# A three-block network on one core: order of ScalarE, VectorE and bank waits in three seven-product MLPs

## The chip, the cores and the metric

One Trainium2 chip, one core. The time is the device time of one launch in microseconds, the median of the runs; a trace of one profiled execution stands beside it. The kernel works in fp32 precision built from fp32r (rounded) operands: each factor is split into a rounded high part and the rest as low part, and a product is three matmuls (high by high, high by low, low by high).

## The reference

512 tokens of width 1024 go through three networks one after the other; five of their parts are MLPs. Cut to what the change touches:

```
squared_relu_mlp(h, w_in, w_out) = square(relu(h @ w_in)) @ w_out          # first block, twice: mlp0, mlp1 (hidden 4096)
gate, up = h @ w_gate, h @ w_up;  (silu(gate) * up) @ w_down                # second block: ffn1, ffn2 (hidden 2816); third: ffn3
h = rms_norm(x, g)                 # ahead of mlp0, mlp1, ffn1, ffn2
mod = silu(c) @ w_ada + b_ada      # conditioning vector of the third block, 1024 -> 6 * 1024
```

The change touches mlp1, ffn1 and ffn3. Between mlp1 and ffn1 nothing stands; ahead of ffn3 stands the third block's first layer norm.

## The kernel before, in words

Activations are kept turned, 128 features by 512 tokens a tile. Each engine has its own program, written out in order by hand, and engines meet only at semaphores (`e.wait_ge`, named by `P`, `C`, `D`, `G` for TensorE, ScalarE, VectorE, GpSimd). SyncE issues all weight loads in one order (`sync`), into three raw slabs in turn: load i waits until the slab of load i - 3 has been read (`raw_free`). GpSimd goes through the same list in `gpsimd`.

An MLP's hidden tiles are worked in groups of four, of which the last of ffn1 and ffn3 has two. Group 0 is done in the ordinary way (`lin`), by TensorE under two-tile steps `p0` = 0 and 2. From group 1 on the three MLPs named use a seven-product (Strassen-Winograd) form: a 1024x256 weight block times 512 tokens is cut 2x2, and seven products of half size replace eight. One **step** of TensorE is `pair_pe` (seven products of 12 matmuls with 256 columns, in the order b, a, c, b, m, c, b over three regions in three PSUM banks) and then `outs_pe` (the down projection of the group before: m output tiles of 12 matmuls with 512 columns). mlp1 has 14 steps with m = 4; ffn1 and ffn3 have 16 steps with m = 2, a gate and a value step in turn, and 2 with m = 4. A step takes 3 + m of the six banks of ring `ps`, each freed by who read it last.

Round the products stands this work. Steps are counted from 0 in each MLP; s is the one that TensorE is in.
- **GpSimd**: `pair_sums_pool` makes the four sums S1, S3, S2, S4 of the weight blocks of a coming pair; `outs_low_pool` makes the low parts of the m output tiles.
- **ScalarE**, `paired_act` for step s: seven high parts of the weight blocks of step s + 1 (`pair_high_act`, a generator, so that `some(high, n)` issues n of them; order A11, A12, S1, S2, A22, S4, S3); m high parts of the down weights of step s (`outs_high_act`); four copies of partial sums out of PSUM (`pair_parts_act`, in the order P1, P5, U2, P4); and two high parts of the hidden tiles or two Silu (`hidden`). Product 3 of TensorE waits for P1, product 5 for P5, product 6 for U2.
- **VectorE**, `paired_dve` for step s: the m adds of the down results of step s - 1 into x; seven low parts of the weights of step s + 1, which free that slab; the hidden low parts; `pair_first_dve` and `pair_second_dve`, which free banks 0 and 1 of the pair; `made`.
- **The conditioning slabs.** In mlp0, mlp1 and ffn1 w_ada is multiplied by the way in 36 parts: parts 0 and 1 of each three load a 1 MB slab (`ada_pe`) and VectorE reads it in four instructions into `macc` (`ada_dve`); part 2 is eight small matmuls of TensorE in a bank of `ps` and one small add. In mlp1 a part belongs to every step, in ffn1 to every second.
- **The opening.** `token_sums_dve` makes four sums of the tokens from ScalarE's scaled copies (`pairs_begin_act`); `pairs_high_act`, `pairs_low_dve`, `pairs_open_act` and `pairs_open_dve` split them and the first pair's weights. `roots_act` and `roots_dve` make rb, 1 / rms of each token. In ffn3 the copies are made in the layer norm.

The order of ScalarE in one step, as the kernel before has it (lines 1901 to 1917):

```
some(parts, opens)
self.outs_high_act(a, o)
some(high, 1)
some(parts, not opens)
some(high, 1 if opens else 2)
... hidden or Silu ...
some(parts, 1); some(high, 2); some(parts, 1); some(high, 1); some(parts, 1); run(high)
```

Of the kernel before, what the change touches and what calls it, by code (L numbers as in the profile page):

```python
# [221 lines left out]
class Net:  # L222
# [152 lines left out]
    def pair_pe(self, e, key, W, c0, after=None, first=False):  # L375
# [6 lines left out]
        self.pair_at[s] = i, q  # L382
        banks = []
        for n in range(3):
            bank, free = self.ps.take(key, n)
            e.wait_ge(*free)
            banks.append(bank)
        a, c, b, m = banks[0][:, 0:256], banks[0][:, 256:512], banks[1][:, 0:256], banks[2][:, 0:256]
        for n, out in enumerate((b, a, c, b, m, c, b)):
            e.wait_ge(*D.at("low", s, n))  # L390
            if first and n in (2, 3, 4, 6):
                e.wait_ge(*D.at(key[0], "tokens", n))
            if n == 3:
                e.wait_ge(*C.at(key, "P1"))
            elif n == 5:
                e.wait_ge(*C.at(key, "P5"))
            elif n == 6:
                e.wait_ge(*C.at(key, "U2"))
            hi, lo = self.piece(self.whi, q + n), self.piece(self.wlo, q + n)
            for k in range(4):  # L400
                xh, xl = self.token_block(n, k)
                e.mm(out, hi[:, k, :], xh, k == 0 and n in self.OPENS, False)
                e.mm(out, hi[:, k, :], xl, False, False)
                t = e.mm(out, lo[:, k, :], xh, False, k == 3 and n in self.CLOSES)
            t.then_inc(*P.up(key, "product", n))
            self.piece_free[q + n] = P.now()
# [1349 lines left out]
    def mlp_pe(self, e, name, gate, up, down, nt, T, ada, between=None, opening=None, last=None):  # L1756
# [39 lines left out]
        for g in range(len(groups) + 1):  # L1796
# [3 lines left out]
            if g < len(groups):  # L1800
                first(g)
                if g == len(groups) - 1:
                    self.P.mark("used", name)
                if ada:
                    self.ada_pe(e)
# [82 lines left out]
    def paired_act(self, a, name, gated, T, g, groups):  # L1888

        D, some = self.D, self.some  # L1890
        hidden = self.hidden_high_act if gated else self.relu_squares_act
        for j, kind, p0, s, o, before, opens, ends, _ in self.pair_steps(name, gated, g, groups):
# [5 lines left out]
            else:  # L1898
                last = "made" if gated else "h"
                parts = self.pair_parts_act(a, key, *(T["gt"][i] for i in pair), *(D.at(name, last, g - 1, i) for i in pair))  # L1900
            some(parts, opens)
            self.outs_high_act(a, o)
            some(high, 1)
            some(parts, not opens)
            some(high, 1 if opens else 2)
            if before:
# [5 lines left out]
            some(parts, 1)  # L1912
            some(high, 2)
            some(parts, 1)
            some(high, 1)
            some(parts, 1)
# [5 lines left out]
    def paired_dve(self, d, name, gated, T, g, groups, add, ada):  # L1922
# [30 lines left out]
        for j, kind, p0, s, o, before, opens, ends, m in self.pair_steps(name, gated, g, groups):  # L1953
# [9 lines left out]
            if before:  # L1963
                for i in range(before[1], before[1] + 2):
                    hidden(d, name, T, before[0], i)
            some(low, 2 if kind == "gate" or not gated else 1)
            self.pair_first_dve(d, key, m1)
# [7 lines left out]
            run(low)  # L1975
            if ada and m * (j + 1) % 4 == 0:
                self.ada_dve(d)
# [5 lines left out]

    def pairs_begin_act(self, a, name, gain):

        a.wait_ge(*self.D.at(f"n{name}", 7))
        for k in range(8):
            a.f(self.tok_t["v"][k // 4][:, k % 4, :], self.x[:, k, :], ACT.Copy, scale=gain(k)).then_inc(
                *self.C.up(name, "token value", k))

    def pairs_high_act(self, a, name):
# [52 lines left out]
    def mlp_act(self, a, name, gated, nt, T, rooted, squares, nxt, extra=None):  # L2044
        groups, way = self.mlp_groups(nt), self.pairing.get(name)
        for g in range(len(groups)):
            if extra:
                extra(g)
            if way and g:
                self.paired_act(a, name, gated, T, g, groups)  # L2050
                continue
            if way and way.gain:
                self.pairs_begin_act(a, name, way.gain)
            for p0 in range(0, len(groups[g]), 2):
# [56 lines left out]
    def mlp_dve(self, d, name, gated, nt, T, add, rooted, squares, ada, nxt, turns=None, amid=None):  # L2111
        P, C, D = self.P, self.C, self.D
        groups, way = self.mlp_groups(nt), self.pairing.get(name)
        for g in range(len(groups) + 1):
# [3 lines left out]
            if g < len(groups):  # L2118
                for p0 in range(0, len(groups[g]), 2):
                    if way and p0 == (0 if way.gain else 2):  # L2120
                        self.token_sums_dve(d, name)
                    if way and p0:
                        low = self.pairs_low_dve(d, name)
                    if gated:
# [5 lines left out]
                if way:  # L2130
                    self.pairs_open_dve(d, name, low)
                if ada:
                    self.ada_dve(d)
# [28 lines left out]
    def relu_mlp_act(self, a, l, nxt, last=None):  # L2162
        name = f"mlp{l}"
        self.roots_act(a, f"n{name}", False)
        self.mlp_act(a, name, False, 32, self.mlp1_t[l], True, True, nxt)
        if last:
            last()
        self.barrier(a, self.C, name)

    def relu_mlp_dve(self, d, l, nxt, amid=None):  # L2170
        name = f"mlp{l}"
        self.roots_dve(d, f"n{name}", False)
        add = lambda d, n, bank, out: d.tt(out, self.x[:, n, :], bank[:, :], ADD)
# [399 lines left out]
    def ffn2_act(self, a, name, nxt):  # L2573
        if name == "ffn2":
            a.dma(self.m3["sp"][:, :], self.A["ssm"]).then_inc(*self.small_in["ssm"].up("ssm"))
        self.roots_act(a, f"n{name}", False)
        self.mlp_act(a, name, True, 22, self.mlp1_t[0], True, name == "ffn1", nxt,
# [5 lines left out]

    def ffn2_dve(self, d, name, nxt):
        self.roots_dve(d, f"n{name}", False)
        add = lambda d, n, bank, out: d.stt(out, bank[:, :], 0.5, self.x[:, n, :], MUL, ADD)
# [2330 lines left out]
```

## Time and profile before

| | us |
|---|---|
| median of 3 runs | 3482.66 (3479.57 to 3490.39) |
| the profiled execution | 3486.54 |
| its span in the trace | 3484.60 |
| TensorE busy | 3300.6 (95%) |
| VectorE, GpSimd, ScalarE busy | 2096.4, 1800.4, 1114.4 |
| mean granted TensorE clock | 0.986 |

Busy shares are means over the whole span, and a busy TensorE isn't TensorE at its peak; for this change the stretches of the three MLPs are read one by one (mlp1 about 940 to 1355 us, ffn1 1355 to 1760, ffn3 3128 to 3472).

### The profile page before, as it was taken

To read this page: it belongs to the slowest core of one execution; us is meant where nothing else is said; L and a number is where in the kernel's file an instruction comes from. 1 tells how busy PE (TensorE), PEld (TensorE's weight loads), DVE (VectorE), ACT (ScalarE), POOL (GpSimd) and SP (SyncE) were. 2 spreads that over 40 slices of the span, in tenths; PEclk is the share of its full clock that TensorE was granted. 3 is DMA by queue.
4 is the path that set the end of the run, shared out by engine and by line. 5 is a ranking of instruction groups with operands and counts; after the bars stand their busy time and mean duration, and the time that the engine had idled before them with its cause. 6 is when DMAs were issued, how large, how long until landed. Compare 5 with 4: busy or idle time off the path is not lost.

```text
span 3484.6 us, 51536 instructions
## 1 busy us (share of the span) xinstructions
PE 3300.6 (95%) x21318; PEld 2714.0 (78%) x21318; DVE 2096.4 (60%) x3132; ACT 1114.4 (32%) x2317; POOL 1800.4 (52%) x1387
## 2 busy tenths in 40 slices
PE   8999999999969899789999998899999999999998
PEld 7768788976758787688978778778887776768997
DVE  6554443467477776678763366554345666658775
ACT  2241111357434433344412442110002116234543
POOL 7526567640344446345676100666664744836562
PEclk9999999999989999899999999999999999999999
DMA  5212333220122323233333100432332735412331
GB/s 178 74 37 97 133 124 130 87 79 13 37 97 97 133 97 103 79 103 103 109 99 114 56 2 15 145 98 91 97 97 89 239 110 182 157 55 85 109 113 52
DMA packets 262153, 341.08 MB, mean 98 GB/s; under 512 B 10016, under 2 KB 202784, under 8 KB 259360
## 3 DMA queue, kind: packets, MB, share of 16 engines
q1 hardware_dynamic: 239408, 301.51, 26.7%
q10 hardware_dynamic: 22512, 36.28, 3.0%
q8 instruction: 169, 2.77, 0.3%
q14 instruction: 64, 0.52, 0.0%
HBM read 308.15 MB, written 25.43 MB: 96 GB/s over the span
## 4 chain that ended last, share of the span: by engine, by line
PE 78%; DVE 13%; DMA 4%; ACT 3%; issue 1%; POOL 1%; ACTq 0%; SPq 0%; DVEq 0%; POOLq 0%
PE bank L130 76%; DVE wlo L153 2%; DMA raw<-in_w_mlp_in 2%; DVE macc L163 2%; PE bank L133 2%; DVE scr L153 1%; DMA sq<-gates 1%; DMA raw<-in_ffn_w_up 1%; DVE gt L153 1%; ACT whi L148 0%; DMA raw<-in_ffn_w_gate 0%; DVE x L153 0%; DVE hl L153 0%; DVE gt L163 0%; DVE st L168 0%
## 5 line engine op out<-in xcount | busy, mean ns | idle before, releaser
L153 POOL TENSOR_TENSOR wlo<-raw,whi 128x512 fp32r<-128x512 f32 x762 | 1058.4, 1417 | 350.5 <-ACT whi L148 337.3
L130 PE MATMUL bank<-ah,whi 128*128 128x512 f32 (+1 forms) x2408 | 872.8, 362 | 67.2 <-ACT gt L148 33.1
L160 POOL TENSOR_SCALAR whi<-raw 128x1024 fp32r<-128x1024 f32 x313 | 361.0, 1171 | 1057.9 <-PE bank L130 543.9
L130 PE MATMUL bank<-ah,wlo 128*128 128x512 f32 (+1 forms) x2408 | 863.2, 358 | 0.0
L130 PE MATMUL bank<-al,whi 128*128 128x512 f32 (+1 forms) x2408 | 851.8, 359 | 0.9 <-DVE al L163 0.9
L130 PEld LDWEIGHTS bank<-ah,whi 128*128 128x128 f32 x2408 | 456.6, 190 | 158.7 <-DVE wlo L153 36.9
L130 PEld LDWEIGHTS bank<-al,whi 128*128 128x128 f32 x2408 | 456.4, 190 | 77.4 <-DVE al L163 1.8
L130 PEld LDWEIGHTS bank<-ah,wlo 128*128 128x128 f32 x2408 | 456.1, 189 | 73.8 <-issue 0.2
L130 PE MATMUL bank<-hh,whi 128*128 128x512 f32 x1040 | 412.6, 397 | 0.5 <-DVE hl L153 0.5
L130 PE MATMUL bank<-hl,whi 128*128 128x512 f32 x1040 | 410.9, 395 | 0.0
L130 PE MATMUL bank<-hh,wlo 128*128 128x512 f32 x1040 | 410.8, 395 | 0.0
L148 ACT ACTIVATE whi<-raw 128x512 fp32r<-128x512 f32 x336 | 204.7, 626 | 313.0 <-PE bank L130 130.4
L153 DVE TENSOR_TENSOR wlo<-raw,whi 128x512 fp32r<-128x512 f32 x200 | 214.3, 1087 | 89.3 <-ACT whi L148 89.2
L130 PEld LDWEIGHTS bank<-hh,whi 128*128 128x128 f32 x1040 | 195.2, 188 | 48.2 <-issue 2.2
L130 PEld LDWEIGHTS bank<-hh,wlo 128*128 128x128 f32 x1040 | 195.0, 187 | 47.6
L130 PEld LDWEIGHTS bank<-hl,whi 128*128 128x128 f32 x1040 | 195.2, 188 | 44.8
L130 PE MATMUL bank<-h,whi 128*128 128x256 f32 x600 | 176.2, 294 | 45.9 <-ACT gt L148 39.2
L130 PE MATMUL bank<-l,whi 128*128 128x256 f32 x600 | 173.7, 289 | 0.0
L130 PE MATMUL bank<-h,wlo 128*128 128x256 f32 x600 | 173.5, 289 | 0.0
L163 DVE SCALAR_TENSOR_TENSOR x<-bank,x 128x512 f32<-128x512 f32 x112 | 74.5, 685 | 141.0 <-PE bank L130 140.7
L130 PEld LDWEIGHTS bank<-h,whi 128*128 128x128 f32 x600 | 118.9, 198 | 49.6 <-ACT gt L148 36.0
L153 POOL TENSOR_TENSOR sq<-raw 128x512 f32<-128x512 f32 x50 | 78.2, 1564 | 145.1 <-DMA raw<-in_w_mlp_in 67.2
(484 smaller groups left out, 5459.3 us busy)
## 6 DMA issues: line engine op xcount, KB each, us to landing
raw<-in_w_in SPq DMA_DIRECT2D x34, 1024.0 KB, 5.3
raw<-in_w_mlp_in SPq DMA_DIRECT2D x32, 1024.0 KB, 5.6
raw<-in_w_mlp_out SPq DMA_DIRECT2D x32, 1024.0 KB, 7.6
raw<-in_w_ada SPq DMA_DIRECT2D x24, 1024.0 KB, 5.4
raw<-in_ffn_w_gate SPq DMA_DIRECT2D x22, 1024.0 KB, 5.4
raw<-in_ffn_w_up SPq DMA_DIRECT2D x22, 1024.0 KB, 5.4
raw<-in_w_ffn_in SPq DMA_DIRECT2D x22, 1024.0 KB, 6.2
raw<-in_w_out SPq DMA_DIRECT2D x16, 1024.0 KB, 5.5
```

Of the source, the lines that this page charges most:

```text
L130: return self.eng.matmul(out, lhsT, rhs, start=start, stop=stop, skip_group_check=True)
L133: return IDLE if self.eng is None else self.eng.transpose(out, src, ident)
L148: return self.eng.activation(out, src, func, scale=scale, **kw)
L153: return IDLE if self.eng is None else self.eng.tensor_tensor(out, a, b, op)
L160: return self.eng.tensor_scalar(out, a, s1, s2, op0, op1)
L163: return IDLE if self.eng is None else self.eng.scalar_tensor_tensor(out, a, s, b, op0, op1)
```

## The change

In all three MLPs:
- `pair_pe` takes its three banks at once but waits for them singly: bank 1 ahead of product 0, bank 0 ahead of product 1, bank 2 ahead of product 4.
- `paired_act`: P1 is copied first in every step. In the first step (`opens`) no high part of the next pair stands ahead of the last copy P4; in the others the numbers of high parts between the copies are 1, 0, 2, 2 and the rest, where they were 1, 2, 2, 1 and the rest.
- `paired_dve`: a part of the conditioning that reads a slab is done after the hidden low parts, in the middle of the step, where it stood at the step's end. Part 2 stays at the end.

In mlp1 and ffn1:
- group 0 has no part of the conditioning any more; all later parts move one place back (a load in the list too).
- ScalarE's eight scaled copies of the tokens and VectorE's four token sums stand ahead of the root, where they stood behind it.

```diff
--- before.py
+++ after.py
@@ -380,13 +380,11 @@
         s, self.n_pair = self.n_pair, self.n_pair + 1
         q = self.pieces(7)
         self.pair_at[s] = i, q
-        banks = []
-        for n in range(3):
-            bank, free = self.ps.take(key, n)
-            e.wait_ge(*free)
-            banks.append(bank)
+        banks, free = zip(*(self.ps.take(key, n) for n in range(3)))
         a, c, b, m = banks[0][:, 0:256], banks[0][:, 256:512], banks[1][:, 0:256], banks[2][:, 0:256]
         for n, out in enumerate((b, a, c, b, m, c, b)):
+            if n in (0, 1, 4):
+                e.wait_ge(*free[{0: 1, 1: 0, 4: 2}[n]])
             e.wait_ge(*D.at("low", s, n))
             if first and n in (2, 3, 4, 6):
                 e.wait_ge(*D.at(key[0], "tokens", n))
@@ -1801,7 +1799,7 @@
                 first(g)
                 if g == len(groups) - 1:
                     self.P.mark("used", name)
-                if ada:
+                if ada and not way:
                     self.ada_pe(e)
             if g:
                 second(g - 1)
@@ -1898,11 +1896,9 @@
             else:
                 last = "made" if gated else "h"
                 parts = self.pair_parts_act(a, key, *(T["gt"][i] for i in pair), *(D.at(name, last, g - 1, i) for i in pair))
-            some(parts, opens)
+            some(parts, 1)
             self.outs_high_act(a, o)
-            some(high, 1)
-            some(parts, not opens)
-            some(high, 1 if opens else 2)
+            some(high, not opens)
             if before:
                 for i in range(before[1], before[1] + 2):
                     hidden(a, name, T, before[0], i)
@@ -1910,9 +1906,9 @@
                 for i in pair:
                     self.paired_silu_act(a, name, T, g, i)
             some(parts, 1)
-            some(high, 2)
+            some(high, 0 if opens else 2)
             some(parts, 1)
-            some(high, 1)
+            some(high, 0 if opens else 2)
             some(parts, 1)
             run(high)
             if ends:
@@ -1963,6 +1959,10 @@
             if before:
                 for i in range(before[1], before[1] + 2):
                     hidden(d, name, T, before[0], i)
+            part = ada and m * (j + 1) % 4 == 0
+            if part and self.ada_d % 3 < 2:
+                self.ada_dve(d)
+                part = False
             some(low, 2 if kind == "gate" or not gated else 1)
             self.pair_first_dve(d, key, m1)
             if kind == "gate":
@@ -1973,7 +1973,7 @@
             self.pair_second_dve(d, key, m2)
             made(kind, p0, p0 + 1, m2)
             run(low)
-            if ada and m * (j + 1) % 4 == 0:
+            if part:
                 self.ada_dve(d)
         if ends:
             for i in (p0, p0 + 1):
@@ -1981,12 +1981,20 @@
                 hidden(d, name, T, g, i)
             adds(g - 1, 8 - m + 2, m - 2)
 
-    def pairs_begin_act(self, a, name, gain):
-
+    def pairs_begin_act(self, a, name):
+
+        if name not in self.pairing:
+            return
+        gain = self.pairing[name].gain
         a.wait_ge(*self.D.at(f"n{name}", 7))
         for k in range(8):
             a.f(self.tok_t["v"][k // 4][:, k % 4, :], self.x[:, k, :], ACT.Copy, scale=gain(k)).then_inc(
                 *self.C.up(name, "token value", k))
+
+    def pairs_begin_dve(self, d, name):
+
+        if name in self.pairing:
+            self.token_sums_dve(d, name)
 
     def pairs_high_act(self, a, name):
 
@@ -2049,8 +2057,6 @@
             if way and g:
                 self.paired_act(a, name, gated, T, g, groups)
                 continue
-            if way and way.gain:
-                self.pairs_begin_act(a, name, way.gain)
             for p0 in range(0, len(groups[g]), 2):
                 if way and p0:
                     high = self.pairs_high_act(a, name)
@@ -2117,9 +2123,9 @@
                 continue
             if g < len(groups):
                 for p0 in range(0, len(groups[g]), 2):
-                    if way and p0 == (0 if way.gain else 2):
-                        self.token_sums_dve(d, name)
                     if way and p0:
+                        if not way.gain:
+                            self.token_sums_dve(d, name)
                         low = self.pairs_low_dve(d, name)
                     if gated:
                         self.gated_dve(d, name, T, g, range(p0, min(p0 + 2, len(groups[g]))), p0, rooted, not (way and p0))
@@ -2129,7 +2135,7 @@
                         turns(g)
                 if way:
                     self.pairs_open_dve(d, name, low)
-                if ada:
+                if ada and not way:
                     self.ada_dve(d)
             if g:
                 end = g == len(groups)
@@ -2161,6 +2167,7 @@
 
     def relu_mlp_act(self, a, l, nxt, last=None):
         name = f"mlp{l}"
+        self.pairs_begin_act(a, name)
         self.roots_act(a, f"n{name}", False)
         self.mlp_act(a, name, False, 32, self.mlp1_t[l], True, True, nxt)
         if last:
@@ -2169,6 +2176,7 @@
 
     def relu_mlp_dve(self, d, l, nxt, amid=None):
         name = f"mlp{l}"
+        self.pairs_begin_dve(d, name)
         self.roots_dve(d, f"n{name}", False)
         add = lambda d, n, bank, out: d.tt(out, self.x[:, n, :], bank[:, :], ADD)
         self.mlp_dve(d, name, False, 32, self.mlp1_t[l], add, True, True, True, nxt, amid=amid)
@@ -2573,6 +2581,7 @@
     def ffn2_act(self, a, name, nxt):
         if name == "ffn2":
             a.dma(self.m3["sp"][:, :], self.A["ssm"]).then_inc(*self.small_in["ssm"].up("ssm"))
+        self.pairs_begin_act(a, name)
         self.roots_act(a, f"n{name}", False)
         self.mlp_act(a, name, True, 22, self.mlp1_t[0], True, name == "ffn1", nxt,
                      (lambda g: {2: self.ssm_sines_act, 3: self.ssm_cosines_act}.get(g, lambda a: None)(a))
@@ -2582,6 +2591,7 @@
         self.barrier(a, self.C, name)
 
     def ffn2_dve(self, d, name, nxt):
+        self.pairs_begin_dve(d, name)
         self.roots_dve(d, f"n{name}", False)
         add = lambda d, n, bank, out: d.stt(out, bank[:, :], 0.5, self.x[:, n, :], MUL, ADD)
         if name == "ffn2":
```

## Rows read from the trace of the kernel before

**Rows 1.** The page: engines; the chain that ended last, by engine.

```profile
PE 3300.6 (95%) x21318; PEld 2714.0 (78%) x21318; DVE 2096.4 (60%) x3132; ACT 1114.4 (32%) x2317; POOL 1800.4 (52%) x1387
...
PE 78%; DVE 13%; DMA 4%; ACT 3%; issue 1%; POOL 1%; ACTq 0%; SPq 0%; DVEq 0%; POOLq 0%
```

**Rows 2.** Stretches in mlp1, ffn1, ffn3: length; busy PE, PEld, DVE, ACT, POOL; PEclk; DMA.

```profile
1014.58:1309.08 294.50, 266.31 (x1617) 235.54 (x1617) 215.65 (x241) 119.54 (x228) 135.98 (x96) 0.98 0.34 115
1437.72:1613.32 175.60, 151.04 (x989) 139.59 (x988) 136.12 (x147) 65.74 (x136) 89.42 (x57) 0.93 0.31 100
3178.26:3409.26 231.00, 231.00 (x1621) 214.49 (x1620) 171.25 (x193) 112.22 (x226) 136.16 (x92) 1.00 0.32 104
```

**Rows 3.** TensorE in mlp1: start us, length, what, [idle before].

```profile
1040.77 0.36 PE L130 MATMUL bank<-ah,whi 128*128 128x256 f32 x1 [1.54 <-DVE x L153]
...
1187.87 0.36 PE L130 MATMUL bank<-ah,whi 128*128 128x256 f32 x1 [1.54 <-DVE x L153]
...
1197.84 0.40 PE L130 MATMUL bank<-hh,whi 128*128 128x512 f32 x1
...
1209.04 0.28 PE L130 MATMUL bank<-ah,whi 128*128 128x256 f32 x1
```

**Rows 4.** TensorE at the openings: mlp1, ffn1 (three rows), ffn3.

```profile
970.51 0.55 PE L130 MATMUL bank<-ah,whi 128*128 128x256 f32 x1 [6.84 <-DVE wlo L153]
...
998.01 0.55 PE L130 MATMUL bank<-ah,whi 128*128 128x256 f32 x1 [17.79 <-ACT gt L148]
...
1381.66 0.79 PE L130 MATMUL bank<-ah,whi 128*128 128x512 f32 x1 [3.72 <-DVE gt L153]
...
1426.31 0.55 PE L130 MATMUL bank<-ah,whi 128*128 128x256 f32 x1 [11.55 <-ACT gt L148]
...
1432.12 0.40 PE L130 MATMUL bank<-hh,whi 128*128 128x512 f32 x1
...
3169.81 0.55 PE L130 MATMUL bank<-h,whi 128*128 128x256 f32 x1 [5.18 <-ACT gt L148]
```

**Rows 5.** ScalarE, opening of mlp1 and two steps in it.

```profile
953.17 5.01 ACT L148 ACTIVATE v<-x,par 128x512 f32<-128x512 f32 x8
...
994.08 1.15 ACT L148 ACTIVATE whi<-raw 128x512 fp32r<-128x512 f32 x2 [18.03 <-DMA raw<-in_w_mlp_in]
...
1042.45 0.39 ACT L148 ACTIVATE gt<-bank 128x256 f32<-128x256 f32 x1 [3.02 <-PE bank L130]
1042.73 0.62 ACT L148 ACTIVATE whi<-raw 128x512 fp32r<-128x512 f32 x1
...
1068.74 0.63 ACT L148 ACTIVATE whi<-raw 128x512 fp32r<-128x512 f32 x1 [8.86 <-DMA raw<-in_w_mlp_in]
```

**Rows 6.** VectorE: opening of mlp1; a contended and a lone low part; a slab read.

```profile
953.31 3.35 DVE L175 RECIPROCAL rb<-rb 128x512 f32<-128x512 f32 x1 [6.99 <-ACT rb L148]
...
963.09 1.28 DVE L163 SCALAR_TENSOR_TENSOR gt<-bank,rb 128x512 f32<-128x512 f32 x2
...
1047.67 0.69 DVE L153 TENSOR_TENSOR wlo<-sq,whi 128x512 fp32r<-128x512 f32 x1
...
1054.75 4.25 DVE L163 SCALAR_TENSOR_TENSOR macc<-raw,mc,macc 128x512 f32<-128x512 f32 x3
...
1072.16 1.77 DVE L153 TENSOR_TENSOR wlo<-sq,whi 128x512 fp32r<-128x512 f32 x1
```

**Rows 7.** SyncE, issue of loads in mlp1.

```profile
986.32 0.50 SPq L123 DMA_DIRECT2D raw<-in_w_mlp_in  x1
...
1059.44 0.51 SPq L123 DMA_DIRECT2D raw<-in_w_mlp_in  x1
```

**Rows 8.** GpSimd: a lone and a contended low part.

```profile
1051.68 1.29 POOL L153 TENSOR_TENSOR wlo<-raw,whi 128x512 fp32r<-128x512 f32 x1 [7.33 <-ACT whi L148]
...
1077.99 1.79 POOL L153 TENSOR_TENSOR wlo<-raw,whi 128x512 fp32r<-128x512 f32 x1 [2.91 <-ACT whi L148]
```

**Rows 9.** The page, loads: KB each, median us from issue to landing.

```profile
raw<-in_w_mlp_in SPq DMA_DIRECT2D x32, 1024.0 KB, 5.6
```

## The prediction

> **What bounds the kernel now.** The page comes first: TensorE is busy for 95% of the span and carries 78% of the chain that ended last, VectorE 13% and loads 4% [rows 1]. So the gain to be had is TensorE's idle time inside the three MLPs, not engine work as such. Second, the busy times by stretch [rows 2] say how much there is. ffn3, 15 steps with m = 2 and no conditioning, is 231.00 us of 231.00 busy at full clock: 15.40 us is the floor of such a step. ffn1's steps 1 to 9 take 175.60 us against 9 x 15.40 + 2 x 0.8 (part 2 of the conditioning, below) = 140.2: 35.4 us lost, at a granted clock of 0.93. For mlp1 the floor is read from one undisturbed step [rows 3]: products from 1187.87 to 1197.84, outs to 1209.04, so 21.17 us. Its steps 1 to 12 take 294.50 us against 12 x 21.17 + 4 x 0.8 = 257.2: 37.3 us lost. Third, the idle times with who ended them [rows 4]: the openings hold 6.84 and 17.79 us (mlp1), 3.72 and 11.55 (ffn1) and 5.18 (ffn3). The long ones all end with a copy of a partial sum by ScalarE, and ScalarE itself was waiting for a load: 18.03 us ahead of 994.08, 8.86 ahead of 1068.74 [rows 5]. It stands in its own order behind a high part of the next pair (`some(high, 1)`), while TensorE wants P1 of this one. And the loads were late because their slab turn came after VectorE's read of a conditioning slab: that read runs from 1054.75 for 4.25 us, and the next pair's load is issued at 1059.44 [rows 6, 7]. So the chain is read, load, high part, P1, product 3.
>
> **Token sums moved up.** In mlp1 ScalarE's eight copies take 5.01 us from 953.17 [rows 5]. x is complete before that, and VectorE is idle for 6.99 us ahead of the reciprocal at 953.31 [rows 6]. Behind it, the wait for the copies and the four sums fill the 6.4 us from 956.66 to the first relu at 963.09. Done ahead, copies and sums (5 us each) end near 955.3, the reciprocal (3.35) at 958.7, the relu comes at 958.9: 4.2 us earlier, and all of the opening with it. TensorE's 6.84 becomes 2.6. In ffn1 the same move makes the 3.72 us vanish: its work runs beside a group 0 that is long enough.
>
> **P1 first, no high part in the opening step.** The wait for P1 (17.79 us in mlp1) goes. What is late next: `outs_pe` of step 0 needs the hidden low parts of tiles 2 and 3, which VectorE makes behind three low parts of pair 1. In mlp1 pair 1's slab is pair 0's. It is issued at 986.32 now [rows 7], behind a slab read of some 3 us, so pair 0 was read at about 983; 4.2 us sooner, less 1 us of contention, is 979.7. With the median of 5.6 us [rows 9] it lands at 985.3; A11, A12, S1 and the hidden parts, high and low, are eight instructions and take about 5.1 more, 990.4. TensorE ended product 4 at 980.2 (998.01 less 17.79); 4.2 sooner, and with products 5 and 6 (held by the last low part) and two rows of outs, it gets there at 981.6: 8.8 us idle in place of 17.79. Gain of mlp1's opening 4.2 + 9.0, less 0.7 for a start at the lower clock level (1.2 in place of 2.4 GHz) that falls on outs in place of products: **12.5** (9 to 17). In ffn1 no conditioning load stands ahead any more, pair 1's slab is there early, and 11.55 becomes about 2.3. After that idle TensorE took 5.81 us (1426.31 to 1432.12) for two products [rows 4], where two of seven in rows 3 take 2.8; most of that comes back too. 3.7 + 9.2 + 2.7 = **15.6** (11 to 18). In ffn3 5.18 goes and about 1 of slow clock, and 1.2 of a new wait for the hidden parts comes: **+5**.
>
> **The steps of mlp1.** Count from TensorE's product 0. P1 can be copied at 1.68 (1042.45 less 1040.77) [rows 3, 5]; ScalarE's next instruction follows 0.28 later, by the rows then a 512-column copy each 0.54 us (0.62 long, overlapping) and a hidden tile 1.2. What it loses by the new order: the down weights' high parts, which it now does beside the outs of the step before, wait behind P1. So they run at 1.96 to 4.2, A11 at 4.1, hidden parts to 7.0, P5 at 7.05 (product 5 wants it at 7.1), A12 to 7.9, and then S1. GpSimd is queued behind that: its four low parts start at 2.6, at 1.29 each lone and 1.79 contended [rows 8], then it makes S1. U2 stands behind S1's high part, at 9.9 to 10.6, where product 6 could start at 8.45. That is a **new wait of 1.5 to 3.2 us in each step**; I take 2.2, near the lone price, as VectorE has little to do just then. The banks: bank 2 waits for an add of VectorE that product 4 wants 5.6 us later, so 0.58 us goes; after part 2 the ring is shifted by one, bank 1 itself waits for an add behind the small one, and of the 1.54 us [rows 3] 0.9 stays, with 0.8 for the eight matmuls. Loads: the slab read in mid-step (4.25 us plus one of about 0.5) no longer ends ahead of a load that the next step wants. In one step of three it now delays the later low parts, so that pair s + 2 is issued at 22 us of the step and lands near 5 of the next, under the S1 wait. 12 x (21.17 + 2.2) + 4 x 1.7 = 287.2 against 294.50: **7.3** (stall 1.5: 16; stall 3.2: -5). Step 13 has no part 2 any more: **+1**.
>
> **The steps of ffn1 and ffn3.** Here only two low parts stand ahead of S1. GpSimd starts at 2.6, S1 ends at 6.5 lone, 7.35 with the contended times; U2 at 7.4 to 8.3, wanted at 8.45: just hidden, and P5 at 4.6 long before. VectorE has 15 instructions a step and 4 more with a slab read, 13 and 18 us with contention; the 5 us of a read are made up in the next step. A pair that needs its forerunner's slab lands up to 6 us into the step: 1 us. Steps 1 to 9: 140.2 + 4 = 144.2 against 175.60: **31.4** (1.7 us a step left: 20; floor: 35). Later in ffn1 two reads fall into steps that lose nothing today: **-1.5**. Step 16 in ffn1 and ffn3 has m = 4 and gets mlp1's wait: **-1.9** each. ffn3's other steps: 0, with no cover against a late S1 (0.3 us a step: -5; nothing to gain, they are at the floor).
>
> GpSimd's low part takes 1.79 in place of 1.29 beside VectorE's work, and VectorE's 1.77 in place of 0.69 [rows 6, 8]. The Trainium skill, "SBUF — State Buffer", section "Who interferes with whom", says that a VectorE instruction with two SBUF inputs and a GpSimd one that reads SBUF lock each other out for a whole instruction. Rows and rule agree on the loser's side for VectorE. By the rule GpSimd could lose a whole VectorE instruction each time, which the change invites, as it moves GpSimd's down parts into the first half of the step; the last rival says what that would give.
>
> **Sum.** 12.5 + 7.3 + 1 + 15.6 + 31.4 - 1.5 - 1.9 + 5 - 1.9 = 67.5 us. The profiled execution took 3486.54 us, of which 3484.60 are the span; it is 3.88 above the median of the runs, 3482.66. I take the difference over to the median: 3482.66 - 67.5 = **3415**.
>
> **Rivals.**
> (a) The steps keep their losses, only the openings gain: 12.5 + 15.6 + 5 = 33, so 3450. That is so if U2 is gated by the load as P1 was: A11, A12 and S1 of the next pair stand ahead of U2, and a slab that lands later than 7 us into a step stops TensorE just as before. For it: 8.86 us of waiting for a load in rows 5. Against it: that load was issued behind a slab read, which is out of the way. Chance 0.15.
> (b) mlp1's steps reach their floor: 12 x 21.17 + 4 x 1.7 = 260.8, 26 us more, 3389. It needs U2 before 8.45, with five GpSimd operations of 1.29 or more from 2.6 on ahead of it: 9.05. Only if ScalarE's down parts didn't wait for P1. Chance 0.08.
> (c) Slower. GpSimd loses time of VectorE's ahead of each operation. At 0.69 each, U2 comes at 13.4 in mlp1 (stall 5.0, 34 us more than I have) and at 9.5 in the 32 steps with m = 2 (1.05 each, 34 us): the gain is gone, no change. It decides from there: at 0.9 each it is 5 x 0.2 x 12 + 3 x 0.2 x 32, 31 us slower, 3514. For it: ffn3 runs without any idle time today because these parts are done a step ahead. Against: the rows show 0.5 at most, and VectorE waits for ScalarE then. Chance 0.05.
> (d) It does nothing that can be told from no change, since the loads and reads only change places: 3483. Against: the waits of rows 4 name ScalarE's copies. Chance 0.03.
>
> **Range and chances.** The forecast has 0.69. The ends of its terms, taken together, would give 15 to 93 us; all at one end is unlikely, and 40 to 90 us is my range: 3393 to 3443. It leaves out (a), half of (b) and (c), (d). A measurement of this kernel can tell about 0.3% from no change, 10.4 us: faster 0.92, same 0.03, slower 0.05.
>
> **What the changed profile would show.** Right: no idle time over 3 us ahead of a copy by ScalarE, but one of about 9 in mlp1's step 0 that ends with a hidden low part (hl); no wait of 3.7 at ffn1's group 0; in mlp1 an idle of about 2 us in each step, between products 5 and 6, ended by a ScalarE copy; steps of 23.4 in mlp1 and 15.4 to 16 in ffn1; ffn3's steps still 15.4. Wrong: idle time ahead of product 6 in ffn3 (then (c)), or ScalarE waiting for loads in every step (then (a)), or mlp1's steps at 21.2 (b).

## The result and the profile after

The changed kernel takes **3457.27 us** (median of 4 runs, 3448.42 to 3460.81) against 3481.52 us before (4 runs): ratio 0.9922, 95% interval 0.9896 to 0.9947. That is 24 to 27 us faster, where 67.5 were forecast and 40 to 90 were the range: the direction is right, the size wrong by a factor of 2.5 to 2.8. The profiled execution took 3448.42 us, the fastest of its four and 9 us under their median (span 3446.5); it is 38 us under the one of before. Of these, 31 lie in the three MLPs. The other 7 lie between ffn1 and ffn3, where the trace of before takes 1429.2 us from ffn1's last step to ffn3's first, and all thirteen other traces 1421.4 to 1423.4. Two of the thirteen, e2 and e11, are the kernel before with one edit inside the MLPs, so I count the 7 us as no effect of the change.

The page of the kernel after, engines and chain:

```profile
PE 3295.1 (96%) x21318; PEld 2701.5 (78%) x21318; DVE 2036.9 (59%) x3132; ACT 1105.2 (32%) x2317; POOL 1803.1 (52%) x1387
...
PE 76%; DVE 11%; POOL 5%; ACT 4%; DMA 2%; issue 1%; ACTq 0%; DVEq 0%; SPq 0%; POOLq 0%
```

Against [rows 1] the loads' share of the chain has halved (4% to 2%), and GpSimd, 1% before, has 5%. The same stretches as in [rows 2], here steps 1 to 12 of mlp1, 1 to 9 and 10 to 16 of ffn1, 1 to 15 and 16 of ffn3 (length; busy PE, PEld, DVE, ACT, POOL; PEclk; DMA share, GB/s):

```profile
1003.60:1299.84 296.24, 267.37 (x1617) 233.45 (x1616) 192.58 (x240) 115.06 (x228) 140.31 (x96) 0.99 0.36 113
1410.11:1565.47 155.36, 146.62 (x989) 134.00 (x988) 118.67 (x144) 65.42 (x135) 82.25 (x54) 0.98 0.34 109
1565.47:1691.07 125.60, 117.58 (x789) 107.00 (x788) 97.76 (x119) 51.94 (x107) 66.97 (x44) 0.99 0.36 118
3131.39:3366.53 235.14, 233.44 (x1621) 215.51 (x1620) 156.71 (x193) 108.89 (x225) 136.69 (x90) 1.00 0.32 104
3366.53:3391.67 25.14, 22.80 (x134) 20.19 (x132) 15.16 (x19) 8.29 (x17) 11.70 (x8) 0.93 0.25 84
```

Term by term, in us (the traces; "before" is the length in the trace of before):

| | before | after | forecast gain | measured gain |
|---|---|---|---|---|
| mlp1, opening to step 1 | | | 12.5 | 11.0 |
| mlp1, steps 1-12 | 294.50 | 296.24 | 7.3 | -1.7 |
| mlp1's end and ffn1's opening | 128.64 | 110.27 | 1 + 15.6 | 18.4 |
| ffn1, steps 1-9 | 175.60 | 155.36 | 31.4 | 20.2 |
| ffn1, steps 10-16 | 113.49 | 125.60 | -3.4 | -12.1 |
| ffn3, step 0 | 22.27 | 18.93 | 5 | 3.3 |
| ffn3, steps 1-15 | 231.00 | 235.14 | 0 | -4.1 |
| ffn3, step 16 | 21.00 | 25.14 | -1.9 | -4.1 |

The openings came in the size that was worked out, 32.7 of 34.1 us. The steps were to give 33.4 net and gave -1.9. TensorE's idle times in the kernel after: mlp1's opening, a wait for U2 and one for a hidden low part in its steps, a value step of ffn1, step 16 of ffn3:

```profile
992.08 0.80 PE L130 MATMUL bank<-hh,whi 128*128 128x512 f32 x1 [9.48 <-DVE hl L153]
...
1014.42 0.39 PE L130 MATMUL bank<-h,whi 128*128 128x256 f32 x1 [1.88 <-ACT gt L148]
...
1092.00 0.50 PE L130 MATMUL bank<-hh,whi 128*128 128x512 f32 x1 [0.73 <-DVE hl L153]
...
1451.87 0.39 PE L130 MATMUL bank<-ah,whi 128*128 128x256 f32 x1 [2.62 <-ACT scr L148]
...
3377.44 0.36 PE L130 MATMUL bank<-h,whi 128*128 128x256 f32 x1 [2.35 <-ACT gt L148]
```

And what ScalarE, GpSimd and VectorE do in mlp1's step 1, which TensorE begins at 1003.60 (first ScalarE, then GpSimd, then VectorE):

```profile
1005.20 0.39 ACT L148 ACTIVATE gt<-bank 128x256 f32<-128x256 f32 x1 [12.54 <-PE bank L130]
1005.48 2.70 ACT L148 ACTIVATE whi<-raw 128x512 fp32r<-128x512 f32 x5
...
1013.47 0.63 ACT L148 ACTIVATE whi<-sq 128x512 fp32r<-128x512 f32 x1 [2.12 <-POOL sq L153]
1014.00 0.37 ACT L148 ACTIVATE gt<-bank 128x256 f32<-128x256 f32 x1
```

```profile
1006.25 5.51 POOL L153 TENSOR_TENSOR wlo<-raw,whi 128x512 fp32r<-128x512 f32 x4 [14.77 <-ACT whi L148]
1011.72 1.72 POOL L153 TENSOR_TENSOR sq<-raw 128x512 f32<-128x512 f32 x1
```

```profile
1014.13 1.20 DVE L153 TENSOR_TENSOR wlo<-sq,whi 128x512 fp32r<-128x512 f32 x1 [1.82 <-ACT whi L148]
1015.25 3.48 DVE L153 TENSOR_TENSOR hl<-gt,hh 128x512 fp32r<-128x512 f32 x2
```

Counted from the start of the step, P1 is copied at 1.6 us, GpSimd's four low parts run until 8.2 and its sum S1 until 9.8; the high part of S1 follows at 9.9 and U2 at 10.4. That chain is as forecast. What the forecast didn't follow is the lower half: VectorE's low part of S1 and, behind it in VectorE's order, the two hidden low parts, done at 1018.73, 15.1 us into the step. In every second step of mlp1 `outs_pe` wants them in that same step; in four of the twelve steps TensorE waits for them, 0.60 to 0.73 us each.

### The profile page after: what moved, and what is told of

Its sections match the earlier page's. It is cut to its first block, busy times and chain, and to the rows that moved or that the text cites. A ratio compares the mean times of both kernels' runs of the same rounds, so it can differ in the third digit from the quotient of the medians.

```text
span 3446.5 us, 51330 instructions
## 1 busy us (share of the span) xinstructions
PE 3295.1 (96%) x21318; PEld 2701.5 (78%) x21318; DVE 2036.9 (59%) x3132; ACT 1105.2 (32%) x2317; POOL 1803.1 (52%) x1387
## 4 chain that ended last, share of the span: by engine, by line
PE 76%; DVE 11%; POOL 5%; ACT 4%; DMA 2%; issue 1%; ACTq 0%; DVEq 0%; SPq 0%; POOLq 0%
PE bank L130 74%; POOL wlo L153 3%; DVE wlo L153 2%; PE bank L133 2%; ACT whi L148 1%; DVE hl L153 1%; DVE scr L153 1%; POOL sq L153 1%; DMA raw<-in_ffn_w_gate 1%; ACT gt L148 1%; POOL whi L160 1%; DVE macc L163 0%; DVE st L168 0%; DMA raw<-in_w_mlp_in 0%; ACT ah L148 0%
## 5 line engine op out<-in xcount | busy, mean ns | idle before, releaser
L153 DVE TENSOR_TENSOR wlo<-raw,whi 128x512 fp32r<-128x512 f32 x200 | 179.3, 901 | 145.9 <-ACT whi L148 145.7
L148 ACT ACTIVATE whi<-raw 128x512 fp32r<-128x512 f32 x336 | 195.6, 620 | 30.3 <-DMA raw<-in_ffn_w_gate 18.0
L153 DVE TENSOR_TENSOR wlo<-sq,whi 128x512 fp32r<-128x512 f32 x100 | 104.2, 1045 | 87.8 <-ACT whi L148 87.2
```

Source lines behind the costliest of these rows:

```text
L148: return self.eng.activation(out, src, func, scale=scale, **kw)
L153: return IDLE if self.eng is None else self.eng.tensor_tensor(out, a, b, op)
```

## The experiments

Two theories. **T1**: a late S1 is what the new order of ScalarE costs, and the gain of the change comes from the slab read in mid-step. **T2**: late slabs bound the steps; the order of ScalarE is right. Ratios are to the kernel before, run beside them. Differences to the changed kernel are of medians that weren't run side by side, and the changed kernel's own interval is 9 us to either side (its four runs lie 12 us apart), so differences of 10 us or so are read from the traces.

### e1: down parts ahead of P1 again

```diff
-            some(parts, 1)
+            some(parts, opens)
             self.outs_high_act(a, o)
+            some(parts, not opens)
             some(high, not opens)
```

> The changed kernel with one thing moved: in all but the opening steps ScalarE makes the high parts of the down weights ahead of P1 again (the order is down parts, P1, A11, ...). Theory T1 (the new wait for U2 comes from the down parts behind P1: they hold up GpSimd's low parts and with them the sum S1 that stands ahead of U2): the wait of 1.86 us ahead of product 6 goes, mlp1's steps 1 to 12 take about 268 us in place of 296, ffn3's steps 1 to 15 take 231 in place of 235.1 and step 16 takes 21 in place of 25.1, some 40 to 50 us less than the changed kernel in all, about 3412. Theory T2 (late slabs of the next pair bound the steps): the wait moves from U2 to a load, mlp1's steps stay over 285 us, the whole is within 10 us of the changed kernel, about 3450.

Measured 3406.40 us, ratio 0.9787 (0.9771 to 0.9804), 51 us under the changed kernel. The same five stretches:

```profile
1002.88:1270.33 267.45, 258.09 (x1618) 229.78 (x1616) 205.40 (x244) 117.53 (x228) 135.79 (x96) 1.00 0.38 127
1379.03:1529.74 150.71, 144.55 (x989) 133.39 (x987) 132.34 (x147) 66.12 (x135) 86.19 (x54) 0.98 0.33 111
1529.74:1651.49 121.75, 118.41 (x788) 108.61 (x789) 108.83 (x121) 54.37 (x109) 74.75 (x46) 0.97 0.36 124
3094.98:3325.98 231.00, 231.00 (x1622) 214.47 (x1620) 161.88 (x194) 109.40 (x227) 142.45 (x92) 1.00 0.32 105
3325.98:3346.98 21.00, 21.00 (x134) 18.79 (x132) 13.25 (x17) 8.82 (x17) 12.78 (x9) 1.00 0.28 101
```

In the step that begins at 1071.81, GpSimd's S1, then ScalarE's high part of S1 and U2:

```profile
1075.15 1.29 POOL L153 TENSOR_TENSOR sq<-raw 128x512 f32<-128x512 f32 x1 [3.94 <-DMA raw<-in_w_mlp_in]
```

```profile
1078.81 0.62 ACT L148 ACTIVATE whi<-sq 128x512 fp32r<-128x512 f32 x1
1079.33 0.37 ACT L148 ACTIVATE gt<-bank 128x256 f32<-128x256 f32 x1
```

U2 is copied 7.5 us into the step in place of 10.4, ahead of product 6. All T1's numbers for the steps (268, 231, 21) are met. The place of the down parts alone is worth 51 us by the medians, 47 by the ratios, 44 by the traces.

### e2 and e3: ScalarE's new order alone, and everything but it

e2 is the kernel before with the new `paired_act`; e3 the changed kernel with the old one:

```diff
-            some(parts, 1)
+            some(parts, opens)
             self.outs_high_act(a, o)
-            some(high, not opens)
+            some(high, 1)
+            some(parts, not opens)
+            some(high, 1 if opens else 2)
...
             some(parts, 1)
-            some(high, 0 if opens else 2)
+            some(high, 2)
             some(parts, 1)
-            some(high, 0 if opens else 2)
+            some(high, 1)
```

> The kernel before with ScalarE's new order in paired_act alone. T1: the openings gain the waits for P1 (some 25 us over the three), the steps of mlp1 gain nothing, since their wait moves to U2, and ffn3 loses 8 us as in the changed kernel; 3460 to 3468. T2: the old slab reads at the step's end keep each load late, P5 and U2 wait for it, and the gain is under 10 us, 3475.

> The changed kernel with the old order of ScalarE in paired_act; slab reads, token sums and bank waits stay as changed. T1: the loads come early enough now, so the old order costs little in the steps: no wait for S1 ahead of U2, ffn3's steps at 231.0 again, mlp1's near 275; the openings lose some 15 us against the changed kernel; in all 3440, better than the changed kernel. T2: P1 waits for the load behind A11 again as in the kernel before, 3470.

e2: 3513.36 us, ratio 1.0091 (1.0076 to 1.0107), **32 us slower** than before; both theories missed it. Its steps 1 to 12 of mlp1 take 312.54 us, and its opening of mlp1 gives next to nothing (step 1 starts 42.9 us after product 0, 44.1 before): the slab read still stands ahead of pair 1's load and the hidden parts behind it. That is the likely reason; no run takes it apart. e3: 3404.18 us, ratio 0.9782 (0.9768 to 0.9797), **53 us faster than the changed kernel**, beyond what T1 gave it (by the traces 46; the changed kernel was traced in its fastest run). So the new order costs 32 us on the old kernel and about 50 on the new. e3's stretches, the first four:

```profile
1003.69:1265.04 261.35, 257.26 (x1617) 230.10 (x1616) 199.81 (x240) 120.22 (x228) 131.99 (x96) 1.00 0.40 133
1376.21:1526.87 150.66, 143.48 (x990) 132.65 (x989) 131.38 (x147) 65.46 (x134) 84.80 (x53) 0.99 0.35 116
1526.87:1647.62 120.75, 116.86 (x789) 107.86 (x788) 106.69 (x119) 54.97 (x109) 74.26 (x46) 0.97 0.36 118
3093.32:3324.98 231.66, 231.66 (x1622) 215.18 (x1621) 170.83 (x193) 112.36 (x226) 136.18 (x91) 1.00 0.32 103
```

With A11 ahead of P1, as before, mlp1's steps are at 21.8 us on average, 33 us under before in all: the load that A11 waits for is there.

T1 had e3's openings 15 us behind those of the changed kernel; that missed. mlp1's step 1 starts at 1003.69 us in e3 and at 1003.60 in the changed kernel. Over the three openings the gain on the kernel before is, by the traces:

| | mlp1 | mlp1's end and ffn1 | ffn3 | sum |
|---|---|---|---|---|
| changed kernel | 11.0 | 18.4 | 3.3 | 32.7 |
| e3, without ScalarE's new order | 10.9 | 17.5 | -0.2 | 28.2 |
| e2, with ScalarE's new order alone | 1.2 | 1.8 | 3.3 | 6.4 |
| e12 (below), e3 with a part of the conditioning in group 0 | 2.2 | 7.8 | -0.1 | 9.9 |

So nearly all of the gain in the openings of mlp1 and ffn1 comes from the empty group 0 and the earlier token sums, and only that of ffn3 from ScalarE's order.

### e5, e6, e7, e12: the other parts, each taken back from e3

```diff
# e5: the slab read at the end of the step
-            if part and self.ada_d % 3 < 2:
-                self.ada_dve(d)
-                part = False
# e6: all three banks ahead of product 0
+        for f in free:
+            e.wait_ge(*f)
...
-            if n in (0, 1, 4):
-                e.wait_ge(*free[{0: 1, 1: 0, 4: 2}[n]])
# e7: the calls of pairs_begin_act and pairs_begin_dve back behind the root
# e12: a part of the conditioning in group 0
-                if ada and not way:
+                if ada:
```

> The changed kernel with the old order of ScalarE (as e3) and besides with the slab reads of the conditioning at the end of the step again. Token sums, bank waits and the missing part in group 0 stay. T1 (the gain of the change is the slab read, which stood ahead of the next pair's load; ScalarE's copies were only where the wait showed): most of e3's gain goes, 40 to 50 us slower than e3's 3404, about 3450. T2 (the openings and the banks carry it): within 15 us of e3.

> e3 with all three banks waited for ahead of product 0 again. T1: bank 2 then waits for an add of VectorE in two of three steps of mlp1 (0.58 us each in rows 3's steps) and after part 2 0.6 us more; 5 to 10 us slower than e3. T2 (with reads in mid-step VectorE is late at the step's end, so the bank waits matter more): 15 us or more slower.

> e3 with the token copies and sums behind the root again in mlp1 and ffn1. T1: mlp1's opening 3 to 4 us and ffn1's group 0 3.7 us later: 7 us slower than e3, 3411. T2 (the opening waits for a load anyway, so this is hidden): within 2 us of e3.

> e3 with a part of the conditioning in group 0 again (so a slab load and its read ahead of pair 1's load in the openings). T1: mlp1's opening 3 us and ffn1's up to 6 us longer, 3410. T2 (the load of pair 1 waits for pair 0 in any case): within 3 us of e3, 3404.

| | us | ratio to before (95%) | worth beside e3 |
|---|---|---|---|
| e5, read at the end | 3461.08 | 0.9944 (0.9928 to 0.9961) | 57 |
| e6, banks together | 3416.71 | 0.9819 (0.9805 to 0.9834) | 13 |
| e7, sums behind the root | 3414.85 | 0.9808 (0.9794 to 0.9823) | 11 |
| e12, part in group 0 | 3416.04 | 0.9816 (0.9799 to 0.9833) | 12 |

All four fall on T1's side, each with a larger price than T1 gave (40 to 50, 5 to 10, 7, and 6 us). The interval of e7 overlaps that of e3 (0.9768 to 0.9797), but its trace has the loss where T1 put it: 2.9 us by mlp1's step 1, 5.6 between mlp1's steps and ffn1's product 0. By the traces e12 loses 18 us in the openings and 5 in ffn1's steps 1 to 9, and wins 7 back in its steps 10 to 15.

Who waited in steps 1 to 12 of mlp1 (us in total, times, longest), e5 and then the changed kernel:

```profile
ACT whi L148 <- DMA raw<-in_w_mlp_in: 72.0, 12, 8.8
...
PE bank L130 <- ACT gt L148: 21.2, 12, 3.4
```

```profile
ACT whi L148 <- POOL sq L153: 48.3, 24, 2.5
...
PE bank L130 <- ACT gt L148: 21.8, 15, 1.9
...
PE bank L130 <- DVE hl L153: 2.7, 4, 0.7
```

TensorE's waits name the same pair of engines with nearly the same sum, 21 to 22 us. What ScalarE itself waited for tells them apart: in e5 a load, in the changed kernel GpSimd's sums. The wait says who came last, not why.

### e11: the slab read in mid-step alone, in the kernel before

> The kernel before with the slab read of the conditioning in mid-step and nothing else. T1: this alone brings most of what the parts beside ScalarE's order bring, 45 to 55 us of the 76, 3430. T2 (it works only with the bank waits and the empty group 0): under 30 us, 3455.

3434.05 us, ratio 0.9867 (0.9851 to 0.9883): 46 us faster. One statement moved ten lines up in `paired_dve` beats the whole change by about 20 us (23 by the medians, 19 by the ratios).

### e4, e9, e10: who waits for the late S1

e4 puts the hidden low parts ahead of the low parts of A12 and S1 (in the opening ahead of A11 too), e9 puts U2 ahead of the high part of S1, e10 does both; the down parts stay behind P1 in all three.

```diff
# e4, in paired_dve
-            some(low, 3)
+            some(low, 0 if opens else 1)
             if before:
                 ... hidden ...
+            some(low, 3 if opens else 2)
# e9, in paired_act
-            some(high, 0 if opens else 2)
+            some(high, 0 if opens else 1)
             some(parts, 1)
-            some(high, 0 if opens else 2)
+            some(high, 0 if opens else 3)
```

> The changed kernel with the two hidden low parts of a step moved ahead of VectorE's low parts of A12 and S1 (in the opening step ahead of all three). T1 (TensorE's waits for hl stand behind S1's low part): the waits ended by hl go, 9.5, 2.6 and 3.3 us in the three openings and about 8 us in the steps; bank 0 then is the next in mlp1's opening and gives back about 4; 3438 to 3445. T2 (hl is late because of load and port, not of the order): under 5 us less than the changed kernel, 3453.

> The changed kernel (down parts behind P1 as changed) with one high part in place of two between P5 and U2, so that U2 stands ahead of the high part of S1; three follow it. T1 (S1 is late behind the down parts; it has two victims, U2 on ScalarE and the hidden low parts on VectorE, which stand behind S1's low part): the wait of 1.86 ahead of product 6 goes, but in every second step of mlp1 the outs wait for hl, some 3 us, since those parts are no earlier; about 15 us less than the changed kernel, 3440. T2 (U2 is the only victim): 30 us less or more, 3425.

> e9 and besides the hidden low parts ahead of VectorE's low parts of A12 and S1 (as in e4). T1: both victims of a late S1 are out of its way, so most of what e1 gave comes back although the down parts still stand behind P1: mlp1's steps near 22, about 3415 to 3420. T2 (GpSimd is late in the step as such, and the loads and later parts hang on it too): within 10 us of e9.

e4: 3444.11 us, ratio 0.9896 (0.9881 to 0.9911), 13 under the changed kernel. e9: 3447.35, ratio 0.9907 (0.9891 to 0.9922), 10 under. Both intervals overlap that of the changed kernel (0.9896 to 0.9947), so neither gain is clear of noise. e10: **3405.91**, ratio 0.9791 (0.9772 to 0.9810), 51 under, which is. Steps 1 to 12 of mlp1 in e4 and in e10, as above:

```profile
1000.72:1307.74 307.02, 274.56 (x1618) 241.65 (x1616) 221.62 (x241) 114.81 (x228) 147.58 (x96) 0.96 0.35 112
```

```profile
1001.74:1276.04 274.30, 260.80 (x1618) 230.43 (x1617) 216.11 (x239) 114.86 (x228) 145.22 (x96) 1.00 0.38 123
```

The changed kernel takes 296.24 there, e9 293.61. So for mlp1's steps e4 alone is 11 us worse (its waits for U2 grew from 21.8 to 27.8 us; why wasn't tried; its openings are 8.5 us shorter), e9 alone 3 better, and the two together 22 better: S1 has two waiters, and with one helped the other holds TensorE. TensorE's waits in steps 1 to 12 of mlp1, e9:

```profile
PE bank L130 <- DVE hl L153: 11.0, 9, 1.7
PE bank L130 <- DVE gt L153: 5.3, 4, 1.5
PE bank L130 <- ACT gt L148: 4.1, 3, 2.0
```

From 21.8 the waits for ScalarE fall to 4.1, but hl rises from 2.7 to 11.0 and a bank that VectorE frees adds 5.3. In e10 no wait for hl is left there. e1 and e10 are two different ways round the same sum, and both get back most of what the new order costs; that is the strongest evidence for T1. That their times agree within 1 us is luck: e10's steps 1 to 12 of mlp1 are 7 us longer than e1's (267.45), and its openings, where it moves the hidden parts too, are 8 us shorter. S1's lateness is not cured in e10, and 7 us of it still show.

### e8: e1 with the opening's hidden parts first

```diff
-            some(low, 3)
+            some(low, 0 if opens else 3)
             if before:
                 ... hidden ...
+            some(low, 3 if opens else 0)
```

> e1 (down parts ahead of P1) and besides in the three opening steps VectorE's two hidden low parts ahead of its low parts of the next pair. T1: the waits for hl in the openings go; as in e4 3 to 3.5 us less in mlp1's and ffn1's opening and 2 in ffn3's, 8 us less than e1: 3398, faster than both kernels. T2 (bank 0, whose reader stands behind, takes the wait's place in full): same as e1, 3406.

3399.47 us, ratio 0.9765 (0.9751 to 0.9780), 2.3% under before and the lowest of all. It isn't clear of e1 or e3: the intervals overlap. ffn3's opening gains 3.5 us on e1. In mlp1's opening T2 holds: a bank that VectorE frees takes the place of hl in full:

```profile
1000.73 0.80 PE L130 MATMUL bank<-hh,whi 128*128 128x512 f32 x1 [9.41 <-DVE gt L153]
```

## Why the prediction was wrong

**Right.** TensorE's idle times in the openings: 2.6 forecast for the 6.84 us (3.51 measured), 8.8 of waiting for hl (9.48), 3.72 gone, 2.3 in ffn1 (2.62). The new wait for U2 in mlp1: 2.2 forecast, 1.85 to 1.88 measured in nine of twelve steps, U2 at 10.4 us of the step against 9.9 to 10.6. That mlp1 would not reach its floor, and that step 16 of ffn1 and ffn3 would get a new wait. Token sums: 4.2 + 3.7 forecast, 9 to 11 measured for the part in e7.

**Right in size, not in cause: the openings.** The prediction puts their gain under "P1 first" and reads the 17.79 and 11.55 us as waits for P1. They stand ahead of the 61st matmul of the step, product 5, so they are waits for P5; ffn3's 5.18 stands ahead of the 73rd, product 6, and is a wait for U2. P1 was copied first in the opening steps already (`some(parts, opens)`). And e3, with ScalarE's old order, keeps 28.2 of the 32.7 us. What the sum also named, that no slab read stands ahead of pair 1's load any more, did the work in mlp1 and ffn1. That the new order seemed to pay for itself there was luck.

**The step that failed is the one on the steps.** They were to give 33.4 us and gave -1.9. The terms that were mis-sized:

- *mlp1, steps 1 to 12: 287.2 forecast, 296.24 measured.* The waits were sized well: 30.0 us forecast (12 x 2.2 + 4 x 0.9), 28.9 measured, of which 21.8 are for U2 and P5 and 2.7 for the hidden parts that the forecast didn't follow. What it had at nothing is that TensorE's busy time grows with the stops: 267.37 us against a floor of 257.2 with part 2. The first matmuls behind a stop take longer (0.39 us at 1014.42, where 0.28 is usual), and the granted clock was 0.99. In e1, with most of the stops gone, the busy time is 258.09.
- *ffn1, steps 1 to 9: 144.2 forecast, 155.36 measured.* "A pair that needs its forerunner's slab lands up to 6 us into the step: 1 us" was too little. VectorE's last low part of the pair, the load that it frees, and ScalarE's A11, in ffn1's step 3 that starts at 1442.03:

```profile
1443.56 0.68 DVE L153 TENSOR_TENSOR wlo<-raw,whi 128x512 fp32r<-128x512 f32 x1
```

```profile
1444.27 0.37 SPq L123 DMA_DIRECT2D raw<-in_ffn_w_gate  x1
```

```profile
1449.88 0.63 ACT L148 ACTIVATE whi<-raw 128x512 fp32r<-128x512 f32 x1 [4.81 <-DMA raw<-in_ffn_w_gate]
```

  A11 comes 7.85 us into the step and stands ahead of P5; where 1 us was reckoned, 2.62 came [1451.87 above]. Four value steps of ffn1 have such a wait, of 1.46 to 2.98 us. The load goes out 2.24 us into the step. The same load in e3 (step 3 from 1407.98) and in e10 (from 1414.76):

```profile
1406.85 0.37 SPq L123 DMA_DIRECT2D raw<-in_ffn_w_gate  x1
```

```profile
1416.85 0.37 SPq L123 DMA_DIRECT2D raw<-in_ffn_w_gate  x1
```

  So the new order makes this load 3.4 us later. The hidden parts behind S1 are not why, since e10 has them ahead and its load is as late (2.09 us into the step); S1's own low part and the rest of VectorE's order behind it are left, and no run takes these apart. In step 5 the load is late in every order (1.4 to 2.6 us into it) and the step long in e1 and e3 too (20.1 and 21.4 us). Of the 11.2 us over the forecast, e1 and e3 still have 6.5: that share is the load's, T2's, and about 4.7 the order's.
- *ffn1, steps 10 to 15: 1.5 us of loss forecast, 8.0 measured* (100.45 us against 92.48). This isn't the order's: e3 has 7.3. With a part left in group 0 (e12, and e11) there is none, 92.48. Moving the parts one place later puts slab reads beside these steps, and in step 11 A11 waits for its load (ScalarE comes to it 8.15 us into the step, 7.34 in e3).
- *Steps with m = 4 and m = 2.* "Just hidden" was worth 0.15 us of cover in the steps with m = 2. ffn3's became 15.50, every fourth 16.3 with a wait for hl, 4.1 us in all. Each step 16 lost 4.1, not 1.9: in ffn3's the wait for U2 is 2.35 us, as GpSimd's four low parts took 5.96 us there, and TensorE's busy time is 1.8 us up (22.80 for 21.00) at a granted clock of 0.93.

**The attribution.** The rows' "ended by ScalarE's copy" [rows 4] was traced to the load behind it, and then the cure of the copy was still credited as the key to the steps. e3 and e11 show that with the load in time the old order costs next to nothing in mlp1 (0.65 us of waits for ScalarE in e3's steps 1 to 12), and e3's steps gain 50 us without the new one. Nothing in the forecast asked what each part was worth if the others stood. It did book 30 us for the new order's waits (12 x 2.2 and 2 x 1.9), but against gains that didn't need the order; measured, it costs 46 to 53.

**The rivals.** (a) has nearly the number, 3450: the openings gained 32.7 and the steps kept their losses. Its mechanism, a copy gated by the load, holds in ffn1's four value steps, where the copy is P5; in mlp1 it is GpSimd's sum [1013.47 above]. (b) asked for "only if ScalarE's down parts didn't wait for P1": e3, where they don't, takes 261.35 against 260.8. e1 takes 267.45, with 0.84 to 1.10 us of waiting for a bank that VectorE frees in every third step and one wait for a load of 2.33 in step 1. (c) had a mechanism close to the one that costs the time, GpSimd's work moved into the crowded part of the step, but asked for 0.69 us of contention on each operation before it would matter, and so got 0.05. The low parts lost 0.1 to 0.2 us each, and the order was a loss all the same.

**The port.** The rule of the Trainium skill that two such instructions lock each other out for a whole one, "SBUF — State Buffer", sections "SBUF: two separate sides" and "Who interferes with whom", agrees with the traces on VectorE's side. Two hidden parts take 3.48 us beside GpSimd's sums, 1.28 where GpSimd is idle (e1, from 1081.57). On GpSimd's side less was lost in the chains that matter: four low parts took 5.51 and 5.96 us, 1.38 and 1.49 each, against 1.29 alone, where a VectorE low part takes 0.69. Single GpSimd low parts elsewhere in the changed kernel took up to 2.28 us.

**Open.** How the 7.85 us in ffn1's value steps could be shortened wasn't tried, nor whether mlp1's opening can be freed of bank 0. Nor was the order with the part left in group 0 and all else as in e3 split further: e12 says only that the empty group 0 gains 18 us in the openings and loses 7 later.

## What to carry to other kernels

When a wait disappears into a chain, price each link's cure alone, with the others both in and out: here moving the read that held a slab was worth 46 us by itself, and moving the copy that showed the wait was worth less than nothing. In an in-order queue, moving a copy ahead moves all that it now stands ahead of behind a new wait; follow that work through every engine that takes it up, to every reader at the end, not only to the first. ffn3's steps ran without idle time while the down parts were made beside the outs of the step before (231.00 us in before and e1), and lost 4.1 us when they weren't, though ScalarE was busy for only 109 of the 235 us.

## What the runs showed of the hardware

Waits of 1.85 to 1.88 us in nine of twelve steps of mlp1 left TensorE's granted clock at 0.99 on average [the first stretch after], nearly all of it at the 2.4 GHz level. In e4, with twelve waits for ScalarE of 2.1 to 2.3 us in the same steps, it was 0.96, and in ffn1 of the kernel before, with waits of up to 6.2 us, 0.93 [rows 2]. After the 9.48 us wait a 512-column matmul took 0.80 us in place of 0.39. GpSimd's sum S1 of 128x512 took 1.72 us in mlp1's step 1, where an instruction of VectorE ran beside it, and 1.26 in ffn3's step 16, where none did.
